# Memory attention of two heads per unit in two stages, and the dense pieces of one of them spread over its units

## The reference, cut to what matters

```
q  = rms_norm(qm.reshape(S, 4, 64), mem_q_norm)
k  = rms_norm(km.reshape(256, 4, 64), mem_k_norm)
om = softmax(q @ k.T * 64 ** -0.5, over the 256 keys) @ v        # each head
y  = concatenate([o, om]) * silu(gate)                           # gate: 1024 wide, h @ w_in
x  = x + y @ w_out
```

## Time and profile before

| | us |
|---|---|
| median of 3 runs | 2430.24 (2428.81 to 2434.48) |
| the profiled execution | 2427.65, span 2425.9 |
| TensorE busy | 2265.5 (93% of the span) |
| VectorE busy | 1214.3 (50%) |
| ScalarE busy | 918.1 (38%) |
| mean granted TensorE clock | 0.971 of full |

### The profile page before, as it was taken

The page is one execution under the profiler, slowest core; times in us unless marked ns, Lnnn a source line. Parts: engine busy times, 40 slices in busy tenths (PEclk is TensorE's granted clock), DMA queues, the critical chain, the costliest instruction groups (busy, mean ns, idle before and its releaser), DMA issues. The chain is left out here.

```text
span 2425.9 us, 35262 instructions
## 1 busy us (share of the span) xinstructions
PE 2265.5 (93%) x14388; PEld 1567.8 (65%) x14388; DVE 1214.3 (50%) x2144; ACT 918.1 (38%) x1644; POOL 46.4 (2%) x36
## 2 busy tenths in 40 slices
PE   6999998899999999999889999998999978999898
PEld 4664444488888766544346888886876556977456
DVE  4633345566662374244456666425455763524344
ACT  4423333433333343233344333334255553314452
POOL 2000001000000020000000000000000000000000
PEclk8999999999999999999999999999999989999699
DMA  4101111122222121111012222222221102221000
GB/s 177 46 27 48 57 48 35 36 103 89 103 87 104 70 70 37 37 53 53 36 36 70 93 99 87 104 71 110 87 72 51 36 18 87 105 93 64 1 1 35
DMA packets 23920, 159.79 MB, mean 66 GB/s; under 512 B 3024, under 2 KB 3664, under 8 KB 4944
## 3 DMA queue, kind: packets, MB, share of 16 engines
q1 hardware_dynamic: 23760, 157.53, 18.2%
HBM read 155.43 MB, written 2.10 MB: 65 GB/s over the span
## 5 line engine op out<-in xcount | busy, mean ns | idle before, releaser
L654 DVE TENSOR_TENSOR arena_r<-ring,arena_r 128x512 fp32r<-128x512 f32 x428 | 297.7, 702 | 479.3 <-ACT arena_r L645 474.8
L645 ACT ACTIVATE arena_r<-ring 128x512 fp32r<-128x512 f32 x428 | 266.9, 632 | 637.4 <-PE banks L695 601.8
L693 PE MATMUL banks<-oT_r,arena_r 128*128 128x512 f32 x1024 | 425.4, 415 | 18.9 <-DVE arena_r L916 14.0
L695 PE MATMUL banks<-oT_r,arena_r 128*128 128x512 f32 x1024 | 407.1, 398 | 0.0
L694 PE MATMUL banks<-hT_r,arena_r 128*128 128x512 f32 x928 | 368.4, 397 | 0.0
L729 PE MATMUL banks<-hT,ring 128*128 128x512 f32 x544 | 263.0, 612 | 0.0
L693 PE MATMUL banks<-arena_r,arena_r 128*128 128x512 f32 x592 | 238.6, 403 | 13.4 <-DVE arena_r L685 10.8
L694 PE MATMUL banks<-arena_r,arena_r 128*128 128x512 f32 x624 | 246.3, 395 | 0.0
L693 PEld LDWEIGHTS banks<-oT_r,arena_r 128*128 128x128 f32 x1024 | 194.2, 190 | 79.5 <-DVE arena_r L916 16.6
L695 PE MATMUL banks<-arena_r,arena_r 128*128 128x512 f32 x592 | 232.8, 393 | 0.0
L695 PEld LDWEIGHTS banks<-oT_r,arena_r 128*128 128x128 f32 x1024 | 193.8, 189 | 47.0
(11 more groups left out here) (383 smaller groups left out, 3029.2 us busy)
## 6 DMA issues: line engine op xcount, KB each, us to landing
ring<-weights SPq DMA_DIRECT2D x142, 1024.0 KB, 4.8
xT<-x_features SPq DMA_DIRECT2D x2, 1024.0 KB, 6.2
arena<-memory SPq DMA_DIRECT2D x2, 1024.0 KB, 4.7
y_features<-xT SPq DMA_DIRECT2D x8, 256.0 KB, 2.0
const<-constants SPq DMA_DIRECT2D x1, 1088.0 KB, 7.7
const<-constants SPq DMA_DIRECT2D x1, 512.0 KB, 8.5
arena<-positions SPq DMA_DIRECT2D x1, 256.0 KB, 2.7
small<-small_vectors SPq DMA_DIRECT2D x2, 68.5 KB, 6.4
```

The costliest lines, as they stand in the source:

```text
L645: act.activation(hi, self.stream.block(b, n), ACT.Copy).then_inc(self.chip.sem("hi_ready"), 1)
L654: vec.tensor_tensor(lo[:, 0:n * P], self.stream.block(b, n), hi[:, 0:n * P].bitcast(F32), ALU.subtract).then_inc(self.chip.sem("lo_ready"), 1)
L693: pe.matmul(out, w_hi, hi, start=k == 0, stop=False)
L695: ins = pe.matmul(out, w_lo, hi, start=False, stop=k == nk - 1)
```

## The change: what it does

1. `memory_units` makes 8 units in place of 16: both heads of a tile for one block of 128 queries. Each has two scores (one for each half of the partitions, in banks of their own), and a unit counts as `two_heads`. Transposes of both heads go into one bank and are copied by one 512-wide instruction; the values are made as two matmuls side by side for each of the two key blocks, one into each half of the output's partitions. VectorE scales each head by its own reciprocal.
2. In `diff_stage` the loop thus has 32 units, and the 60 gate pieces are spread over its first 33 iterations.
3. In `late_prepare_stage` 12 gate pieces come ahead of the loop, three ahead of each sum and three behind the last, and 52 are spread over its first ten iterations; the three squares are made first; the scores get four banks, the transposes one and the output one; the query's gain is negated and holds the scale, so that the maximum is one VectorE instruction less; the silu is made unit by unit with Tanh, whose table also serves the exponential, so that the table is changed once.
4. `late_out_stage` multiplies the memory tiles with 0.5 as well.

The diff, without the lines that only wrap a pair in a list or pass AHEAD to Pace:

```diff
@@ -1814,11 +1816,15 @@
     def __init__(self, chip, units, banks, work, stat, negated=False):
         self.chip, self.units, self.negated = chip, units, negated
         self.scores = Banks(banks, chip.sem("s_ready"), chip.sem("p_ready"))
-        wide = max(len(u.pairs) for u in units)
+        halves = all(u.two_heads and u.narrow for u in units)
+        wide = 1 if halves else max(len(u.pairs) for u in units)
         self.prob = [[chip.t(work + wide * i + j) for j in range(wide)] for i in range(4)]
+        if halves:
+            self.prob = [[tile[:, 0:S // 2], tile[:, S // 2:S]] for tile, in self.prob]
         n = work + 4 * wide
-        self.probT = [chip.t(n), chip.t(n + 1)]
-        self.end = n + 2
+        turned = 2 if any(u.two_heads and not u.narrow for u in units) else 1
+        self.probT = [[chip.t(n + turned * i + j) for j in range(turned)] for i in range(2)]
+        self.end = n + 2 * turned
         assert self.end <= ARENA
         self.stat = stat
         self.lag = 2
@@ -1844,19 +1850,25 @@
                     pe.wait_ge(chip.sem(name), count)
                 masked = self.negated and u.mask is not None
                 banks = [self.scores.fill(pe) for _ in u.pairs]
-                for bank, (q, k) in zip(banks, u.pairs):
-                    ins = pe.matmul(bank[:, 0:u.keys], q, k, start=True, stop=not masked)
-                    if not masked:
-                        ins.then_inc(chip.sem("s_ready"), 1)
+                parts = len(u.pairs[0])
+                for part in range(parts):
+                    for bank, pair in zip(banks, u.pairs):
+                        q, k = pair[part]
+                        ins = pe.matmul(bank[:, 0:u.keys], q, k, start=part == 0, stop=part == parts - 1 and not masked)
+                        if part == parts - 1 and not masked:
+                            ins.then_inc(chip.sem("s_ready"), 1)
                 for bank in banks if masked else ():
                     pe.matmul(bank[:, u.keys - P:u.keys], chip.eye_b, u.mask, start=False, stop=True).then_inc(chip.sem("s_ready"), 1)
             if 0 <= i - self.lag - 1 < n:
                 u = self.units[i - self.lag - 1]
                 pe.wait_ge(chip.sem("w_ready"), i - self.lag)
-                bank = chip.T.fill(pe)
-                for b in range(u.keys // P):
-                    ins = pe.transpose(bank[:, b * P:(b + 1) * P], self.prob[(i - self.lag - 1) % 4][0][:, b * P:(b + 1) * P], chip.c("ident"))
-                ins.then_inc(chip.sem("t_ready"), 1)
+                for at, w in self.turned(u):
+                    bank = chip.T.fill(pe)
+                    for j in at:
+                        for b in range(u.keys // P):
+                            x = w * (j - at[0]) + b
+                            ins = pe.transpose(bank[:, x * P:(x + 1) * P], self.prob[(i - self.lag - 1) % 4][j][:, b * P:(b + 1) * P], chip.c("ident"))
+                    ins.then_inc(chip.sem("t_ready"), 1)
                 evacs.append(chip.T.filled)
             if 0 <= i - self.lag - 2 < n:
                 u = self.units[i - self.lag - 2]
@@ -1864,12 +1876,21 @@
                     self.obank = chip.O.fill(pe)
                 pe.wait_ge(chip.sem("t_used"), evacs[i - self.lag - 2])
                 nb = u.keys // P
+                probT = self.probT[(i - self.lag - 2) % 2]
                 for b in range(nb):
-                    ins = pe.matmul(self.obank[u.rows, u.cols], u.values(b), self.probT[(i - self.lag - 2) % 2][:, b * P:(b + 1) * P],
-                                    start=b == 0, stop=b == nb - 1)
+                    for j in range(2 if u.two_heads else 1):
+                        rows, values = (u.rows[j], u.values[j]) if u.two_heads else (u.rows, u.values)
+                        p = probT[j][:, b * P:(b + 1) * P] if j < len(probT) and not u.narrow else probT[0][:, (nb * j + b) * P:(nb * j + b + 1) * P]
+                        ins = pe.matmul(self.obank[rows, u.cols], values(b), p, start=b == 0, stop=b == nb - 1, skip_group_check=u.two_heads)
                 if u.last:
                     ins.then_inc(chip.sem("o_ready"), 1)
 
+
+    def turned(self, u):
+
+        if not u.two_heads:
+            return [((0,), 0)]
+        return [((0, 1), u.keys // P)] if u.narrow else [((0,), 0), ((1,), 0)]
 
     def scalar(self, act, a, meanwhile=None):
         chip, n = self.chip, len(self.units)
@@ -1898,9 +1919,11 @@
         chip, n = self.chip, len(self.units)
         if 0 <= i - self.lag - 1 < n:
             u = self.units[i - self.lag - 1]
-            c.turn()
-            c(act.activation(self.probT[(i - self.lag - 1) % 2][:, 0:u.keys], chip.T.take(act)[:, 0:u.keys], ACT.Copy), chip.sem("t_used"))
-            yield True
+            for at, _ in self.turned(u):
+                w = len(at) * u.keys
+                c.turn()
+                c(act.activation(self.probT[(i - self.lag - 1) % 2][at[0]][:, 0:w], chip.T.take(act)[:, 0:w], ACT.Copy), chip.sem("t_used"))
+                yield True
         if 0 <= i - self.lag - 2 < n and self.units[i - self.lag - 2].last:
             u = self.units[i - self.lag - 2]
             c.turn()
@@ -1952,7 +1975,17 @@
         c.turn()
         c(vec.reciprocal(self.col("inv", s), self.col("sum", s)))
         yield True
-        if len(u.pairs) == 2:
+        if u.two_heads:
+            p1 = w[1][:, 0:u.keys]
+            c.turn()
+            c(ts(p, p, self.col("inv", s), None, ALU.mult))
+            yield True
+            c.turn()
+            c(vec.reciprocal(self.col("inv", s + 1), self.col("sum", s + 1)))
+            yield True
+            c.turn()
+            c(ts(p1, p1, self.col("inv", s + 1), None, ALU.mult), chip.sem("w_ready"))
+        elif len(u.pairs) == 2:
             p1 = w[1][:, 0:u.keys]
             c.turn()
             c(vec.reciprocal(self.col("inv", s + 1), self.col("sum", s + 1)))
+
+
 def late_prepare_stage(chip, stream, layer, work):
 
     nc = chip.nc
     chip.start()
     u0, u1 = stream.units("g0", f"g{GATE - 1}")
-    items = [(chip.t(LKM), chip.s("mem_k", layer))] + [(chip.t(LQM + i), chip.s("mem_q", layer)) for i in range(2)]
-    sq, r = [chip.t(work), chip.t(work + 1)], [chip.t(work + 2), chip.t(work + 3)]
+    neg_m = chip.stat[:, 45:46]
+    items = [(chip.t(LKM), chip.s("mem_k", layer))] + [(chip.t(LQM + i), neg_m) for i in range(2)]
+    n = len(items)
+    sq, r = [chip.t(work), chip.t(work + 1), chip.t(work + 2)], [chip.t(work + 3), chip.t(work + 4)]
     sig = [chip.t(LSIG), chip.t(LSIG + 1)]
-    n = len(items)
     h = parts_of_h(chip, "stick", "b")
     split = Split(chip, stream, u0, u1, pairs_of(chip.h_r, 0, 4))
-    jobs = jobs_of(stream, u0, u1)
-    SIG_AFTER = GATE // 2
-    attn = Attention(chip, memory_units(chip, lambda i: chip.t(LMEM + i)), chip.psum[4:6], work + 2, chip.stat)
-    later = Later(jobs[n + 1:])
+    chip.T = Banks(chip.psum[2:3], chip.sem("t_ready"), chip.sem("t_used"))
+    chip.O = Banks(chip.psum[7:8], chip.sem("o_ready"), chip.sem("o_used"))
+    attn = Attention(chip, memory_units(chip, lambda i: chip.t(LMEM + i)), chip.psum[3:7], work + 2, chip.stat, negated=True)
+    ahead = PREPARED * (n + 1)
+    pace = lambda **does: Pace(GATE * KD, len(attn.units) + 2, ahead, **does)
+    ready_chunks = lambda steps: min(len(split.chunks), 4 + steps // 4)
 
     with nc.Block() as block:
         @block.sync
@@ -2534,81 +2573,79 @@
 
         @block.tensor
         def _(pe):
-            def make(job):
-                split_product(chip, pe, split, job[0], h)
-
...
+            for i in range(n):
+                run(PREPARED)
+                bank = chip.T.fill(pe)
+                pe.wait_ge(chip.sem("sq_ready"), i + 1)
+                pe.matmul(bank, chip.c("blk64"), sq[i], start=True, stop=True).then_inc(chip.sem("t_ready"), 1)
+            run(PREPARED)
             pe.wait_ge(chip.sem("kn_ready"), n)
-            attn.tensor(pe, later.on(tensor=make))
-            for job in later.rest():
-                make(job)
+            attn.tensor(pe, pace(tensor=run))
 
         @block.scalar
         def _(act):
             a = Order(act, chip.sem("act_step"))
 
-            def empty(job):
-                split.scalar(act, job[-1])
-                for u in job:
-                    if (u - u0) % SIG_AFTER == SIG_AFTER - 1:
-                        act.wait_ge(chip.sem("dense_used"), u - u0 + 1)
-                        for j in range(u - u0 - SIG_AFTER + 1, u - u0 + 1):
-                            if j >= 2:
-                                act.wait_ge(chip.sem("gate_ready"), j - 1)
-                            a(act.activation(sig[j % 2], chip.t(LG8 + j), ACT.Sigmoid), chip.sem("sig_ready"))
-                        act.preload_act_table_set(EXP_LN)
-
+            def gates(steps):
+                split.scalar_chunks(act, ready_chunks(steps))
+                for g in range(gates.done, steps // KD):
+                    gates.done = g + 1
```

(65 more changed lines are left out.)

48 lines of the change are left out of this document (15 added, 33 removed).

## The result

The changed kernel took 2390.41 us in the median of three runs (2385.41 to 2393.84). The kernel before took 2430.72 beside it; the ratio is 0.983 with an interval of 0.9815 to 0.9846. The same kernel run again gave 2391.04, ratio 0.9825 [0.981, 0.9841]. So it is faster by 37 to 45 us, where 43 had been forecast, and the predicted 2387.2 is 3 us low.

A forecast was written before the change was run, and what follows sets the result against it. TensorE, busy in 93% of the span, was taken as the bound. Gains of 15.5 (differential stage) and 28.4 us (preparing stage), less 1 for hand-overs, give 43: median 2387.2 us, range 2378 to 2402 for 8 of 10, own range 2381 to 2394.

The forecast's parts named there:

- The likeliest case: Both changed stages: 15.5 us gained in the differential and 28.4 in the preparing stage, 2387.2 us in all; chance 0.66.
- A: Memory units in both stages: the two heads do not run side by side, 13.8 us less gain, 2401; chance 0.11.
- B: Preparing stage: it keeps a stretch at half clock, which costs 15 us, 2402; chance 0.09.
- D: Preparing stage: the new mix holds the clock at half throughout, 60 us more, 2446, slower than before; chance 0.03.
- C: Loop iterations: VectorE's lumps ahead of the maxima make TensorE stand 0.5 us each, 2396; chance 0.11 together with E.
- one of the prediction's signs of being wrong: Loops of both stages: the prediction is wrong if TensorE stands behind VectorE there; no size given.
- the half clock of the end: End of the preparing stage: 9.2 units fall from 2.81 to 1.58 us each, 11.3 us gained.
- the middle: Middle of the preparing stage: the shorter half-clock stretch of 3.5 us goes, 1.7 us gained.
- standing: Preparing stage: TensorE's standing falls from 5.2 to 1.6 us, 3.6 us gained.
- the earlier start: Start of the preparing stage: first piece after 2.7 us, where the square kept TensorE 4.1 before; 1.4 us gained.
- changes: Preparing stage: changes between pieces and scores, ten at 0.20 us in the new stage, counted as -1.2 us of gain.
- the 14.0 from which the range was made: Differential stage: gain of 14.0 us if every returning piece costs full time, up to 19.6 if standing is filled; 15.5 taken.

The follow-up runs named there:

- the lump: Kernel with only the differential stage changed, plus gates by Tanh in place of Sigmoid in the old preparing stage, four Tanh and four products together: 2417.51 us, stage 100.36.
- gates in turn: Against the kernel with four Tanh and four products together in the old preparing stage, its last four gates made one by one: 2406.01 us, stage 86.11.
- the uncovered kernel: Changed kernel with single-head units in the preparing stage and its 52 pieces all in the first eight iterations, none beside the last eight units: 2408.56 us, stage 88.0.
- the experiment with the order moved: Changed kernel with the transposes of the earlier unit put ahead of the scores in iterations of two-head units: 2396.04 us, ratio 0.9853.
- The split lump: Changed kernel with VectorE's product of gate g in the differential stage made one iteration behind its tile, not with tile g + 1: 2387.58 us, ratio 0.981.

## Why the prediction was right, and where it was off

**The mechanism and its parts.** The likeliest case came true. A is excluded: scores 0.64 (0.63 put) and values 0.58 (0.58 put) for two heads, without the 0.1 us more that the prediction also names as an estimate. B and D did not come: the clock is 1.00 from 2176.1 us to the stage's end. C shows only as the 5.1 us of standing in the differential part, where the kernel before had 5.6, not as new standing in each iteration. To the letter this meets one of the prediction's signs of being wrong (TensorE stands behind VectorE in the loops); that sign did not allow for the standing that was there before.

**Preparing stage: -28.1 against -28.4.** The first piece comes 2.7 us after the start, as put. The parts can now be read off four kernels: from the lump to gates in turn -14.25 (100.36 to 86.11), the spreading, the new prelude and the scores' four banks -4.34 (to 81.77), two heads per unit -11.1 (to 70.64). That makes 29.7 and not 28.1, since these kernels start from an old stage of 100.36 whose half clock lasted longer than in the kernel before, 98.77. The prediction had 11.3 for the half clock of the end, 1.7 for the middle and 3.6 for standing, 1.4 for the earlier start, -1.2 for changes, which makes 16.8 against 18.6 measured for the first two, 1.6 of it this longer half clock; and 11.9 against 11.1. In the sum for the new stage errors cancel by luck: a unit costs 1.81 us and not 1.67, 1.1 more for the eight, and the half clock at the start lasts 3.4 us and not 5.7, 1.2 less.

**One reason in it was wrong or at least unproved.** The first part said that the clock is low at the end "where the gate pieces are used up". The bare units of the uncovered kernel and those of the kernel with gates in turn ran at 1.00. What the prediction also said, under B, that the stage fell to half clock whenever TensorE had stood two to three us, is what the runs bear out. That the spread pieces were needed for the clock is not so; four Tanh and four products in turn brought 14.25 us without them. Whether pieces behind a stop shorten the half clock stays open. It lasted 3.4 us where pieces followed (stops of 1.97, 2.69 and 2.81 us, and the 4.0 at the start of the changed stage) and 27.3 to 30.7 where bare units did (3.21 and 3.57 us), but no run changes only what follows a stop.

**Differential stage: -12.1 against -15.5; this is the step that was mis-sized.** It is also below the 14.0 from which the range was made. 1.55 us of the 3.4 lie in the memory part, 22.86 us against the 21.3 put. Of that, four transposes behind scores cost 0.59, not 0.46: 0.13 for each of the five units whose transposes fall in this part, 0.65. A price read from a differential unit (0.44) doesn't hold behind plain scores; the experiment with the order moved shows 0.53 behind pieces, so 0.06 of it is the neighbour's and 0.07 the transposes' own. 0.60 is one wait of the fourth unit's transposes for ScalarE's copy of the earlier ones:

```profile
1855.07 0.63 PE L1870 MATMUL banks<-const,arena 128*128 128x128 f32 x4 [0.60 <-ACT arena L1925]
```

The other 0.3 are small: 0.70 for a piece and 0.19 for a change add up to it in part.

0.9 us lie in the differential part and the tail. TensorE's work grew by 5.8, as put (5.9). But its standing went from 5.64 only to 5.08, where I let 1.4 go, and the tail grew by 0.3. The split lump shows why for a part of it: with one product moved out of the lump ahead of the maxima 5.0 us of waits become 2.9. Dense pieces stand ahead of the scores and the wait is behind them, so I read that they can't fill such a stop; no run tests that by itself.

The last 1.0 us is in front of the loop, which the change leaves as it was: the half clock at the stage's start lasted 6.8 us in place of 3.4, first in the kernel before, then in after.

```profile
1773.20:1776.50 3.30, 3.30 (x12) 2.24 (x11) 2.76 (x5) 3.24 (x7) 0.00 (x0) 0.50 0.00 0
```

```profile
1776.80:1783.50 6.70, 5.48 (x19) 4.40 (x20) 3.25 (x5) 5.24 (x9) 0.00 (x0) 0.50 0.39 142
```

The same 1.0 shows in the stick stage (96.34 against 95.29), and in the other profiles either length comes up in these stages with no pattern that follows the edits. I had counted 1 us for all hand-overs.

**The sum.** The stages from the differential one on give 39.0 us by the traces; the medians differ by 40.3 and the ratio gives 41. The forecast of 43 was high mainly by the 3.4 of the differential stage. It stays inside its own range of 2381 to 2394 because the preparing stage, two thirds of the gain, was met within 0.3.

## What to carry over

When TensorE's clock falls at one place, look first at what it did just before: behind a stop of 3.6 us ten units were 1.23 us longer each, and breaking up a lump on VectorE got that back. Try to move a piece of side work by some iterations before moving it to another engine. Take a price of one instruction from a row with the same neighbour, for the change between array forms is part of it.

## What the runs showed of the hardware that was not expected

Once the clock was at 0.50, it stayed there through 26.6 us of memory units alone with TensorE busy all the time, and rose to 1.00 at 2265.5 us, with the last of them. Started at 1.00, the same instructions held 1.00. With pieces or sums behind the stop the clock came back within a few us (the stretches of 5.7 and 3.5 us in the earlier trace rows). A stop of 1.7 us can go either way: in after one of 1.67 us left the clock at 1.00, in the kernel with transposes first it fell behind one of 1.66.

The fp32 products of two heads into different halves of the output's partitions overlap in both orders tried: 0.58 to 0.59 us for all eight records either way, as long as four of one head take.

A GpSimd product beside VectorE lengthens it. In the differential part VectorE's L1997 of 512 columns took 1104 ns in the mean in place of 751, L1994 829 in place of 546, and a maximum read from a bank 691 as before. In the place shown the 384-wide L1997 that takes 0.62 alone took 1.50 and ended 0.4 behind GpSimd's instruction, which looks like waiting for it to end; GpSimd's spans are rough. The Trainium skill ("SBUF — State Buffer", SBUF: two separate sides) calls the port pair of the two engines "an exclusive lock, not a bandwidth split" for an operation with two SBUF inputs against a GpSimd one that reads SBUF; the trace agrees for L1997, which has two, and for the maximum, which reads a bank and did not grow. L1994, which has one, grew too, and no row here says why.
